# Chunk stage of a gated DeltaNet layer: loads of heads spread over the periods, and multiplications into unread banks ahead of the stage

## What is computed

```python
a_mat = where(strict, einsum(kb, k) * decay, 0)
sol = triangular_solve(a_mat + eye, concat(v * beta, kb * exp(gc)), unit_diagonal=True)
u, w = split(sol)
def step(s, inp):                       # over the chunks
    v_new = u_n - w_n @ s
    o = qd_n @ s + qk_n @ v_new
    s = s * gt_n + kt_n.T @ v_new
```

## Time and profile before

| | us |
|---|---|
| median of 3 runs | 2771.13 |
| lowest, highest | 2769.49, 2779.35 |
| the profiled execution's own time | 2773.22 |
| its span in the profile | 2771.4 |
| TensorE matmul busy | 2574.0 (93%) |
| VectorE busy | 1808.1 (65%) |
| ScalarE busy | 1253.1 (45%) |
| GpSimd busy | 1213.0 (44%) |
| mean granted clock of TensorE | 0.965 |

### The profile page before, as it was taken

How to read it: one execution, slowest core, us unless ns; L and a number is a source line. 1 busy time by engine, 2 the same in 40 slices (tenths; PEclk the granted TensorE clock), 3 DMA queues, 4 the chain that set the end, 5 groups by cost and what they waited for, 6 DMA issues and landing times. The chain is left out here.

```text
span 2771.4 us, 51972 instructions
## 1 busy us (share of the span) xinstructions
PE 2574.0 (93%) x18313; PEld 2489.4 (90%) x18313; DVE 1808.1 (65%) x2723; ACT 1253.1 (45%) x2169; POOL 1213.0 (44%) x1111
## 2 busy tenths in 40 slices
PE   6999999988987999999999699998998999999995
PEld 6999999988975899999999699998998999998994
DVE  5477777776016788888888567776766777776103
ACT  4566666662013543444544245553544555465102
POOL 1433333436241345555444355555554555573320
PEclk9999999999998999999999689999999999999997
DMA  4122222122113355554445642424244241423113
GB/s 156 46 61 61 61 62 63 57 102 99 46 55 124 87 161 148 167 156 134 137 143 142 183 95 51 119 50 117 65 105 107 50 119 50 119 70 110 46 38 122
DMA packets 243120, 269.27 MB, mean 97 GB/s; under 512 B 86747, under 2 KB 210220, under 8 KB 241276
## 3 DMA queue, kind: packets, MB, share of 16 engines
q1 hardware_dynamic: 242940, 266.96, 33.7%
HBM read 182.59 MB, written 84.33 MB: 96 GB/s over the span
## 5 line engine op out<-in xcount | busy, mean ns | idle before, releaser
L688 PE MATMUL ps<-dn_yhi,dn_whi 128*128 128x348 f32 x1128 | 385.7, 342 | 8.1 <-ACT p_vrow L1588 5.4
L2321 ACT ACTIVATE zz<-ps 104x416 fp32r<-104x416 f32 x560 | 283.6, 516 | 238.9 <-PE ps L2157 237.0
L690 PE MATMUL ps<-dn_yhi,dn_wlo 128*128 128x348 f32 x1128 | 363.3, 322 | 0.0
L689 PE MATMUL ps<-dn_ylo,dn_whi 128*128 128x348 f32 x1128 | 363.3, 322 | 0.0
L2444 DVE TENSOR_TENSOR pp<-ps,level_mask 104x416 fp32r<-104x416 f32 x480 | 275.6, 587 | 131.4 <-PE ps L2157 129.8
L688 PE MATMUL ps<-rg_yhi,rg_whi 128*128 128x348 f32 x912 | 295.7, 324 | 15.2 <-POOL rg_ylo_r L865 6.3
L690 PE MATMUL ps<-rg_yhi,rg_wlo 128*128 128x348 f32 x912 | 295.2, 324 | 0.0
L689 PE MATMUL ps<-rg_ylo_r,rg_whi 128*128 128x348 f32 x912 | 295.2, 324 | 0.0
L2159 PE MATMUL ps<-pp,zz 104*104 104x208 f32 x1440 | 266.4, 295 | 28.0 <-DVE pp L2444 18.6
L2159 PE MATMUL ps<-zz,pp 104*104 104x208 f32 x1440 | 247.7, 282 | 0.0
L2159 PEld LDWEIGHTS ps<-pp,zz 104*104 104x104 f32 x1440 | 186.8, 177 | 49.3 <-issue 28.0
(11 more groups left out here) (362 smaller groups left out, 7099.2 us busy)
## 6 DMA issues: line engine op xcount, KB each, us to landing
c_nq<-nq_scratch SPq DMA_DIRECT2D x160, 169.0 KB
dn_raw<-in_dn_w_in SPq DMA_DIRECT2D x48, 512.0 KB, 4.3
qd<-rows_scratch SPq DMA_DIRECT2D x160, 104.0 KB, 3.1
rg_raw<-in_rg_w_in SPq DMA_DIRECT2D x32, 512.0 KB, 4.5
nq_scratch<-p_nq SPq DMA_DIRECT2D x48, 338.0 KB
p_ex<-rows_scratch SPq DMA_DIRECT2D x32, 422.5 KB
nq_scratch<-p_rn SPq DMA_DIRECT2D x32, 338.0 KB
n_h<-h_scratch SPq DMA_DIRECT2D x16, 520.0 KB, 7.9
```

What stands on the lines that cost most here:

```text
L688: e.matmul(o, whi, mhi[:, t0:t0 + tn], start=(first and k == 0), stop=False)
L689: e.matmul(o, whi, mlo[:, t0:t0 + tn], start=False, stop=False)
L690: ins = e.matmul(o, wlo, mhi[:, t0:t0 + tn], start=False, stop=(last and k == end))
L2321: e.activation(zz[:, b, :, :], ps[0:CH, 2 * b + 1, 0:m4], ACT.Copy).then_inc(zev.sem, 1)
```

## The change

TensorE gets 62 matmuls of 128x512 at the end of `dn_project`, into bank 6 after the last read of it (operands: the split weights and activations that lie there), and 24 matmuls of the identity with the matrix of ones, 128x128 in four passes, into bank 7 as its first instructions in `dn_chunks`, ahead of its first wait. Nobody reads their results.

On SP, `load` is split into its parts. At the start of the stage the systems of steps 0 to 3 go first, then `vrow` of head 0, the decay rows of steps 0 and 1, queries, keys and `krow` of head 0, the systems of steps 4 to 9, `zs` of head 0 and the decay rows of steps 2 to 5. The second head of each turn is loaded in that turn (period 4 `krow`, period 5 queries, keys and `vrow`, period 7 `zs`), the first head of the next turn in periods 6, 7, 9 and 10. The store of a turn's second head moves from behind period 12 to period 4 of the next turn. SP's first turn is written out, and its loop has two turns. The order of the instructions on all other engines stays.

```diff
@@ dn_project, block.tensor
             turn(0, True)
             with e.Fori(1, QK_HEADS) as n:
                 turn(n)
+            e.wait_ge(raw_done.sem, raw_done.at(QK_HEADS, 0))
+            for _ in range(62):
+                e.matmul(ps[:, 6, :], wt.hi[:, 0, 0:P], yhi[0][:, 0:512], start=True, stop=True)
@@ dn_chunks, block.sync
-            def load(n, h):
+            def load(n, h, *which, fresh=False):
                 i = h % 2
-                if h >= 2:
+                if not fresh:
                     e.wait_ge(om.sem, om.at(n, (h - 2) * NC + NC))
                     e.wait_ge(kt_done.sem, kt_done.at(n, (h - 2) * NC + NC))
+                if "z" in which and not fresh:
                     e.wait_ge(gated.sem, gated.at(n, (h - 2) * 5 + 5))
                 hold(e, s.passed)
...
             def store(n, h):
                 e.wait_ge(gated.sem, gated.at(n, 5 * h + 5))
                 hold(e, s.passed)
-                e.dma_start(o_dram.rearrange("a p t -> p a t")[:, bass.ds(n * 4 + 2 * h, 2), :], vo[:, h]) \
-                    .then_inc(o_out[h].sem, 16)
+                e.dma_start(o_dram.rearrange("a p t -> p a t")[:, bass.ds(n * 4 + 2 * h, 2), :], vo[:, h % 2]) \
+                    .then_inc(o_out[h % 2].sem, 16)
...
-            def turn(n, last):
+            SECOND = {4: ("krow",), 5: ("qk", "vrow"), 7: ("z",)}
+            NEXT = {6: ("krow",), 7: ("qk",), 9: ("vrow",), 10: ("z",)}
+
+            def turn(n, last, first=False):
                 for p in range(3, 2 * PAIRS + 3):
+                    if p == 4 and not first:
+                        store(n, -1)
+                    if p in SECOND:
+                        load(n, 1, *SECOND[p], fresh=first)
+                    if p in NEXT and not last:
+                        load(n, 2, *NEXT[p])
                     if p == 8 and not last:
                         store(n, 0)
-                        load(n, 2)
...
-                if not last:
-                    store(n, 1)
-                    load(n, 3)
-
-            for g in (0, 1):
+
+            for g in range(4):
                 load_systems(0, g)
-            load(0, 0)
-            for g in range(2, NC):
+            load(0, 0, "vrow", fresh=True)
+            decay_rows(0, 0), decay_rows(0, 1)
+            load(0, 0, "qk", "krow", fresh=True)
+            for g in range(4, NC):
                 load_systems(0, g)
-            for g in range(6):
+            load(0, 0, "z", fresh=True)
+            for g in range(2, 6):
                 decay_rows(0, g)
-                if g == 1:
-                    load(0, 1)
-            with e.Fori(0, TURNS - 1) as n:
+            turn(0, False, True)
+            with e.Fori(1, TURNS - 1) as n:
                 turn(n, False)
             turn(LAST, True)
@@ dn_chunks, block.tensor
+            for _ in range(24):
+                e.matmul(ps[:, 7, 0:P], c["ident"][:, :], c["ones"][:, :], start=True, stop=True)
             e.wait_ge(eye_done.sem, eye_done.at(0, 2))
```

More of the change, by code:

```diff
@@ L1971, in _ @@
             rows = rows_dram[0].rearrange("(d h) t -> d h t", d=2)
-            def load(n, h):
+            def load(n, h, *which, fresh=False):
                 i = h % 2
-                if h >= 2:
+                if not fresh:
                     e.wait_ge(om.sem, om.at(n, (h - 2) * NC + NC))
                     e.wait_ge(kt_done.sem, kt_done.at(n, (h - 2) * NC + NC))
+                if "z" in which and not fresh:
                     e.wait_ge(gated.sem, gated.at(n, (h - 2) * 5 + 5))
                 hold(e, s.passed)
[L1980 to L1989, removed]
+                if "qk" in which:
+                    e.dma_start(qk[:, i], qk_dram.rearrange("a p t -> p a t")[:, bass.ds(n * 4 + 2 * h, 2), :]) \
+                        .then_inc(qk_in[i].sem, 16)
+                if "krow" in which:
+                    e.dma_start(krow[:, i].rearrange("c k m -> c (k m)").unsqueeze(1),
+                                krow_dram.rearrange("n c x -> c n x")[:, bass.ds(n * 2 + h, 1), :]) \
+                        .then_inc(krow_in[i].sem, 16)
+                if "vrow" in which:
+                    e.dma_start(vrow[:, i].rearrange("c k r m -> c (k r m)").unsqueeze(1),
+                                vrow_dram.rearrange("n c x -> c n x")[:, bass.ds(n * 2 + h, 1), :]) \
+                        .then_inc(vrow_in[i].sem, 16)
+                if "z" in which:
+                    e.dma_start(zs[:, i], z_dram.rearrange("a p t -> p a t")[:, bass.ds(n * 4 + 2 * h, 2), :]) \
+                        .then_inc(z_in[i].sem, 16)
             def store(n, h):
```

## The result

| | before | after |
|---|---|---|
| median, us (8 runs each) | 2775.65 | 2759.47 |
| lowest, highest | 2766.38, 2790.32 | 2756.24, 2769.52 |
| ratio to before, 95% interval | | 0.9944, 0.9927 to 0.9961 |
| profiled execution, its span | 2773.22, 2771.4 | 2766.53, 2764.8 |

The kernel became faster by 16 us (2775.65 - 2759.47), by the interval 11 to 20. The forecast was 34, and 2759.47 lies above its range. The profiled execution of after is one of its slower ones; it is set beside the profile of before stretch by stretch.

A forecast was written before the change was run, and what follows sets the result against it. TensorE was taken as busy nearly everywhere at full clock, so gains come where it waits or runs slowly. Opening 18.4 + jumps 15.7 = 34.1 us; 2773.2 - 34.1 = 2739.1 for the profiled execution, median 2737, range 2731 to 2756.

The forecast's parts named there:

- The 62, cost nothing: Wide matmuls behind the projections: 14.3 us of work, hidden behind SP's wait until its branch at 1561.5.
- The 24, cost 1.6 us, a fall and a return: Head of chunk stage: clock falls, returns while they run, a third at half clock; period 0 starts at 1571.3.
- Period 0, 13.0 us: Chunk stage's first period: 28.3 us falls to 13.0, by full clock and no 3.3 us wait for GpSimd.
- Period 1, 21.1 us with 1 us of stall: Chunk stage's second period, 25.8 us before: 5.7 us go, 1 us of stall for late keys and queries.
- The opening's 18.4 us: Start of chunk stage: third period starts at 1605.4 in place of 1623.81; bounds 15 and 20.5 us.
- The first rival: Opening: clock does not hold through the inverse; opening gains only 1.7 us, total 17.4, median 2754; chance 0.14.
- The jump with no loads beside it, 15.7 us gained: Chunk loop's two jumps back: with loads moved away, their 10.6 and 11.3 us shrink to 3.1 us each.
- The row that the prediction held against this rival: At the jump: SP also stands 8 us behind its own burst, cited against the jump's cost staying unchanged.
- the jump costs what it costs: Rival at the jumps: code is fetched slowly with or without loads, VectorE idles 8 us; gain 18.4, median 2753; chance 0.14.
- The rule that the prediction weighed against this step: At the jump: code and loads share queues, code waits a packet, not a burst; part of VectorE's 7.98 us stays.
- Loads spread over the periods, cost nothing: Chunk stage, SP's queue: heads' loads and stores moved among periods, covered by a 23 us period, no cost.
- late-load rival: Rival: queries and values issued at period 5 land after period 6 starts; slower, 2785; chance 0.02.

The follow-up runs named there:

- 12: Changed kernel without the 62 matmuls at the end of the projections; 2763.14 us, ratio 0.9962.
- 3: Changed kernel with the chunk stage's turns written out on all engines, so no jump back; 2740.40 us, ratio 0.9874.
- 6: Changed kernel with all turns written out on all engines and the last turn's load of gates behind the first out-projection weights; 2732.05 us, ratio 0.9854.
- 7: Changed kernel with VectorE's turns alone written out; 2747.82 us, ratio 0.9903.
- 8: Changed kernel with GpSimd's turns alone written out, by mistake in place of TensorE's; 2761.07 us, ratio 0.9954.
- 10: Changed kernel with the turns of TensorE and VectorE written out; 2738.98 us, ratio 0.9873.
- 2: Kernel before with the 62 and 24 matmuls alone added, SP's order as before; 2775.87 us, ratio 1.0003.
- 5: Changed kernel with the last turn's load of gates moved behind the first out-projection weights; 2756.52 us, ratio 0.9924.
- 9: Changed kernel with TensorE's turns alone written out; 2760.63 us, ratio 0.9959.
- 13: Changed kernel with SP holding back systems and decay rows behind a jump until VectorE's first pp of period 3; 2763.95 us, ratio 0.9960.
- 4: Kernel before with the chunk stage's turns written out on all engines, loads still in a burst; 2750.17 us, ratio 0.9915.

## Why the prediction was wrong, step by step

**The 62, cost nothing.** Right, with 0.1 to 0.2 us to spare before SP's branch. What they are needed for was overrated: 1.6 us of the opening (12).

**The 24, cost 1.6 us, a fall and a return.** In the profile of after there was no fall (5.59 us for 24, though the pause in front was 3.44 us). In 3, 6, 7, 8 and 10 there was one, with 7.22 us for the 24 and pauses of 3.5 to 4.0 us: 1.6 us longer, the predicted size. In 2, 5, 9 and 13 there was none. The length of the pause doesn't decide it: 3.47 us ended in a fall (8), 3.54 us did not (2). At full clock the 24 take 5.59 us, not the 4.9 of the forecast.

**Period 0, 13.0 us.** It took 15.20: 0.81 of it is a wait for `nhr` behind the first step; in 3 it was 14.56. So the rest took 14.39 us, 1.4 more than the forecast. **Period 1, 21.1 us with 1 us of stall.** It took 20.29; `krow` was there at 1586.39, and TensorE had no stall. Period 0 started at 1569.26, 2.0 us before the predicted 1571.3 (0.9 of it is an earlier SP branch), took 2.2 us more, and period 1 took 0.8 less. These errors nearly cancel, which is luck: the third period starts at 1604.75, predicted 1605.4. **The opening's 18.4 us are right** (19.1 in the profile, 18.1 from SP's branch on). Its bounds were added wrongly: by their own terms (2 us more stall and 3.2 more for the 24, or 1 and 1.6 less) they are 13.2 and 21.0, not 15 and 20.5; the result doesn't hang on it. The first rival, a clock that doesn't hold through the inverse, is out: 1.00 from 1584 to 1588, where the earlier trace rows had 0.50.

**The jump with no loads beside it, 15.7 us gained.** This is the step that failed: the two pairs took 117.2 us before and 117.0 after, a gain of 0.2. It took VectorE's 7.98 us for a wait behind the burst and put 1.9 us, from TensorE's jump, in its place. Measured, the burst makes 1.7 us of it a jump. The rest stays, though the DMA engines are nearly idle for its last 2.7 us (6.7 us a jump in 13, with the multiplications' 1.5 us in it). TensorE's 1.9 us were a row of another engine, and no bound for VectorE. The row that the prediction held against this rival, SP's 8 us behind its own burst, was itself a jump's: without one SP goes on at once (4). The rival "the jump costs what it costs" came about, which had 0.14. Nor was the short part gained: the multiplications lengthened TensorE's stall from 1.9 to 3.3 us and VectorE's by 1.5, and the pauses at the jumps still ended in a clock of 0.50, which costs several us more. The forecast priced the 86 new instructions by their run time and not by what they do to the jumps behind them; how they do it isn't shown.

The rule that the prediction weighed against this step, the Trainium skill (DMA: Bandwidth & Descriptors, Queues, rings and completion order), by which rows are served in turn, a packet each, was nearer to the runs than the forecast: of 7.5 us a jump (14.9 / 2) the burst is 1.7. The Trainium skill (Runtime: NRT & Kernel Launch, Instruction fetch mechanics) names the stall of a taken branch as a reason to unroll fully; experiments 3, 4 and 10 agree, with 19 us, 23 us and 20.5 us (4 beside the runs of before on its chip, 2773.29).

**Loads spread over the periods, cost nothing.** Right for six of the seven heads' loads: no wait of TensorE for a head's loads appears. Wrong for the last turn, where the load of gates stands in period 7 ahead of the out-projection weights. The prediction said that the loads stand "in front of that period's systems", and didn't look at what else SP issues in that period. GpSimd waits 2.2 us longer for the weights, is late with `kt`, TensorE pauses 1.88 us, and the clock falls: 5.4 us. That is the late-load rival's mechanism in another place, with another queue member as the victim.

**The sum.** Of the profiles' difference (2773.22 - 2766.53 = 6.7 us) the opening gives 19.1, the pairs 0.2, the last turn -5.4. A period in the middle of the second turn, at 1982.8 us, took 28.10 us where before took 23.40: the clock fell at a change of heads without a jump. That is -4.7. These make 9.2. Of the remaining 2.5, 1.1 is a period of the last turn (24.36 us at 2343.41, before 23.30), and 1.4 lies behind the start of the stage's last period (275.6 us to the end, before 274.2). Such a fall turns up in other profiles too (two in experiment 5, at changes of heads; one in 4, behind the second burst; none in 6). It seems to differ from execution to execution; its cause stays open. The medians differ by 16.2 us and not 6.7, since the profiled execution of after is 7.1 us above its median and that of before 2.4 below its own.

## What to carry to other kernels

A row of another engine is no price for an engine's own jump: where a stall stands beside a burst of loads, write the loop out on the engine whose stall ends last, and find every engine that stalls, since mending one brings out the next. Multiplications that keep the clock up are worth nothing if a later wait drops it again (-1.4 us alone, 9 beside the loads), and those nearest to the work that needs the clock did nearly all. When a load moves to another period, list everything that the queue issues there, the other phase's weights too.

## What was not expected of the chip

A jump back to the start of a long turn stalled VectorE 5.0 to 8.9 us, TensorE 1.7 to 3.7 and ScalarE 2.2 to 2.5, VectorE's still 6.7 us where nothing but the last decay rows was in transfer beside it (13). Multiplications ahead of the loop changed these stalls without being in it: with 0, 24, 62 and 86 of them TensorE's "issue" in the loop was 3.7, 8.9, 10.2 and 6.7 us for both jumps. The Trainium skill (Runtime: NRT & Kernel Launch, Instruction fetch mechanics) says that code is fetched in blocks of a fixed number of instructions, so where the loop begins in its block could matter; no run here varied that alone. TensorE's pauses of 3.4 us at the jumps of after were followed by a clock of 0.50, and in the same execution one of 3.44 us ahead of the 24 was not.
